# Reordering the opening of a two-layer macaron step: a split first modulation load, plain products moved up, a shared scaled x, a copy ahead of squares

## The chip, the cores and the metric

The kernel runs on one core of a Trainium2 chip. The metric is the device time of one execution in microseconds; the median over the runs of a program is compared. The profiler gives one execution of the program, with the span of its instructions and a record for each of them.

## What is computed

The reference is one inference step over two layers. Each layer is a half-step SwiGLU feed-forward block (FFN), a token mixer (differential attention, then multi-head latent attention), and a second half-step FFN. All sub-layers read a modulated RMS norm of the activations, and the modulation comes from a conditioning vector by a large matrix:

```python
def modulation(cond, w_mod, b_mod):
    m = jax.nn.silu(cond) @ w_mod + b_mod
    return m.reshape(cond.shape[0], 1, N_MOD, D_MODEL)

def modulate(x, g, shift, scale):
    return rms_norm(x, g) * (1.0 + scale) + shift

def swiglu(h, w_in, w_out):
    g, u = jnp.split(h @ w_in, 2, axis=-1)
    return (jax.nn.silu(g) * u) @ w_out
...
    x = x + m[2] * (0.5 * swiglu(modulate(x, norm_g[0], m[0], m[1]), w_in[0], w_out[0]))
```

There are 128 context tokens, with one conditioning vector, and 256 latent tokens with another. `D_MODEL` is 1024 and `D_FF` is 2816. Everything is float32. Only the first of these FFNs, and in it the first some 50 us, is touched by the change.

## The kernel before

Activations are held transposed as `x[128, 8, 384]`: eight tiles `k` of 128 features, 384 tokens, of which `LAT` (256 columns) are latent and `CTX` (128 columns) are context. A weight matrix is read from memory in panels; a panel `m` of the FFN's first matrix gives two output tiles (`half` 0 and 1) for each `k`. A float32 product is made of three faster ones: ScalarE (ACT) rounds a panel or an activation to a high part (`w_hi`, `hx_hi`), VectorE (DVE) subtracts to get the low part (`w_lo`, `hx_lo`), and TensorE (PE) adds hi*hi, hi*lo and lo*hi (`mm3`, lines 2367 to 2369).

**The opening** can't have all of this ready at once, since nothing is in SBUF when it starts. Three panels (`SLOTS`) are worked on together, tile `k` by tile `k`, as their data lands. The order of the work on each engine is written out by hand, one list for each engine, and semaphores tie the lists together:

- SyncE (SP) issues all loads of the opening on one DMA queue: `cond`, then the first modulation tile (`load_first(0)`, 1024 KB), x tiles 0 and 1, pieces of the three panels, modulation tiles 1 and 2, x tiles 2 and 3, and so on. The load of x tiles 4 to 7 (`x_in`) is the twelfth of the queue.
- For each `k`, TensorE computes the modulation of that tile: `mod_rows(k)` (line 2476, 16 records) from modulation tile `k`, then ScalarE copies the rows from PSUM to SBUF (`copied(k)`, line 973), then `mod_columns(k)` (line 2488, 4 records) turns them, and VectorE makes the gain from them (`gains_of(k)`, lines 1611 and 1544).
- For each `k`, x is scaled by that gain and multiplied by the three panels. For `k` = 0 that is done as plain float32 (`plain(m, 0, half)`, line 2498, two passes for each product), without a high and a low part. From `k` = 1 on ScalarE makes the high part of the scaled x (`xg_first(k)`, lines 985 and 987), VectorE the low part (`first_xg_low(k)`, lines 1628 and 1764), and TensorE does `tiles(m, k)`.
- Beside that runs the norm: ScalarE squares the eight x tiles (`square(k)`, line 967), VectorE adds them up (`add(k)`, line 1606), and TensorE sums over features (`sum_squares(0)`, line 2380) and later broadcasts the root (`broadcast(0)`). The panel products do not need the norm until their end: the result is scaled by it afterwards.

TensorE's place for `sum_squares(0)` is after `tiles(0, 3)`, behind two waits:

```python
tiles(0, 3)
pe.wait_ge(gains, 9)
sum_squares(0)
```

The ninth gain is the first instruction of `gains_of(4)` on VectorE, which stands behind `add(4)` to `add(7)` there. TensorE begins with `zeros(3)` (line 2521), products of a zero tile that keep it busy until the first data is in.

Of the kernel before, what the change touches and what calls it, by code (L numbers as in the profile page):

```python
# [21 lines left out]
F32 = mybir.dt.float32  # L22
F32R = mybir.dt.float32r
ALU = mybir.AluOpType
ACT = mybir.ActivationFunctionType
# [5 lines left out]
KD = D // P  # L31
KF = FF // P
T = 384
TX = T + 64
LAT = slice(0, 256)
CTX = slice(256, 384)
# [69 lines left out]
def build_step(nc, d, o):  # L106

    ctx = ExitStack()
    with ctx:
        def sem(name):  # L110
            return ctx.enter_context(nc.semaphore(name))
# [194 lines left out]
        wmf_loaded = [sem(f"wmf_loaded{i}") for i in range(KD)]  # L306
        condT_in = sem("condT_in")
        condT_ready = sem("condT_ready")
        first_in = [sem(f"first_in{i}") for i in range(5)]
        rows_ready = sem("rows_ready")  # L310
        rows_copied = sem("rows_copied")
# [353 lines left out]
        def _(sp):  # L665
# [25 lines left out]
            def load_first(k):  # L691
                sp.dma_start(wm_first[:, k], d["w_mod_first"][k]).then_inc(wmf_loaded[k], 16)
# [5 lines left out]
                sp.dma_start(w_raw[:, :, quarter(q)],  # L698
                             d["w_in"][0][0:SLOTS].rearrange("m p c -> p m c")[:, :, quarter(q)]).then_inc(first_in[q], 16)

            load_first(0)
            load_x(slice(0, 2), first_in[0])
            for cols, signal in ((slice(0, 2 * P), first_in[0]), (to_round(0), first_in[4])):
                sp.dma_start(w_raw[:, :, cols],
# [135 lines left out]
        def _(act):  # L840
# [115 lines left out]
            def first_norm():  # L956
# [5 lines left out]
                def square(k):  # L962
                    if k == 2:
                        act.wait_ge(first_in[1], 32)
                    elif k == 4:
                        act.wait_ge(x_in, 16)
                    nc.scalar.activation(squares_all[:, k, :], x[:, k, :], ACT.Square).then_inc(x_squared, 1)
# [8 lines left out]
                def xg_first(k):  # L976
                    if k == 0:
                        act.wait_ge(first_in[0], 32)
                    act.wait_ge(gains, 2 * k + 2)
                    if k < RAW:  # L980
                        nc.scalar.activation(xg_raw[:, k, LAT], x[:, k, LAT], ACT.Copy,
                                             scale=gmul[:, k, 1:2]).then_inc(xg_hi_done, 1)
                        return
                    out = hx_hi[:, k, :]
                    nc.scalar.activation(out[:, T:T + 2], modc[:, k, :], ACT.Copy)
                    for s, seg in SEGS:
                        ins = nc.scalar.activation(out[:, seg], x[:, k, seg], ACT.Copy, scale=gmul[:, k, s:s + 1])
                    ins.then_inc(xg_hi_done, 1)
# [30 lines left out]
                xg_first(2)  # L1019
                copied(3)  # L1020
                xg_first(3)
                square(4)
                square(5)
                copied(4)
                square(6)
                square(7)
                first_high(2)
                xg_first(4)
                copied(5)
# [456 lines left out]
        def _(v):  # L1486
# [109 lines left out]
            def first_norm():  # L1596
# [41 lines left out]
                first_low(0, (0, 1, 2))  # L1638
                add(1)
                gains_of(1)  # L1640
                first_xg_low(1)
                add(2)
                add(3)
                gains_of(2)
# [719 lines left out]
        def _(pe):  # L2364
# [70 lines left out]
            def ffn_in(f, n):  # L2435
# [32 lines left out]
                else:  # L2468

                    def mod_rows(k):  # L2470
                        pe.wait_ge(wmf_loaded[k], 16)
                        if k:
                            pe.wait_ge(rows_copied, k)
                        for i in range(2):
                            for g in range(4):
                                mm = nc.tensor.matmul(ps[32 * g:32 * g + 32, FIRST_ROWS, 0:2 * P],
                                                      condT[:, 4 * i + g, :], wm_first[:, k, 4 * i + g, :],
                                                      start=i == 0, stop=i == 1)
                        mm.then_inc(rows_ready, 1)
# [54 lines left out]
                    plain(0, 0, 0)  # L2534
                    plain(0, 0, 1)
                    plain(1, 0, 0)
                    mod_rows(1)
                    plain(1, 0, 1)
                    mod_columns(1)
                    plain(2, 0, 0)  # L2540
                    plain(2, 0, 1)
                    mod_rows(2)
                    tiles(0, 1)
                    mod_columns(2)
# [644 lines left out]
```

## Time and profile before

| | |
|---|---|
| median of 3 runs | 1514.74 us |
| lowest and highest | 1514.4 and 1515.72 us |
| the profiled execution | 1515.06 us |
| its span | 1513.1 us |
| TensorE busy | 1503.7 us, 99% of the span |
| VectorE, ScalarE busy | 1095.5 us, 676.1 us |
| TensorE busy between 1.90 and 51.00 us | 46.63 us of 49.10 |

The span runs from the first to the last instruction; the rest of the execution's time is around it. An engine's idle time in the profile stands in front of the instruction that ended it, with the instruction or the DMA that released it. Ends of matmuls are modelled, so the idle times of TensorE are good to about a tenth of a microsecond. Times in the trace count from the span's start.

### The profile page before, as it was taken

To read this page: it belongs to the slowest core of one execution; us is meant where nothing else is said; L and a number is where in the kernel's file an instruction comes from. 1 tells how busy PE (TensorE), PEld (TensorE's weight loads), DVE (VectorE), ACT (ScalarE), POOL (GpSimd) and SP (SyncE) were. 2 spreads that over 40 slices of the span, in tenths; PEclk is the share of its full clock that TensorE was granted. 3 is DMA by queue.
4 is the path that set the end of the run, shared out by engine and by line. 5 is a ranking of instruction groups with operands and counts; after the bars stand their busy time and mean duration, and the time that the engine had idled before them with its cause. 6 is when DMAs were issued, how large, how long until landed. Compare 5 with 4: busy or idle time off the path is not lost.

```text
span 1513.1 us, 22073 instructions
## 1 busy us (share of the span) xinstructions
PE 1503.7 (99%) x8874; PEld 1444.6 (95%) x8874; DVE 1095.5 (72%) x1788; ACT 676.1 (45%) x1067; POOL 34.8 (2%) x45
## 2 busy tenths in 40 slices
PE   8999999999999999999999999999999999999999
PEld 5999999988889999999999999999997899999999
DVE  4888899879887878776677887876588876343332
ACT  4633333353686633333363333325458765333221
POOL 0000000000031000000000000000030000000000
PEclk9999999999999999999999999999999999999999
DMA  9556667543133365655445555654331033333333
GB/s 378 225 217 241 246 243 255 185 149 135 73 99 140 131 230 209 236 188 190 169 177 203 215 224 204 239 181 153 115 121 57 5 136 112 139 114 136 101 130 118
DMA packets 53990, 258.02 MB, mean 171 GB/s; under 512 B 6656, under 2 KB 9728, under 8 KB 39168
## 3 DMA queue, kind: packets, MB, share of 16 engines
q1 hardware_dynamic: 51344, 253.13, 46.3%
q10 hardware_dynamic: 2544, 3.48, 0.7%
q8 instruction: 70, 1.15, 0.3%
q14 instruction: 32, 0.26, 0.1%
HBM read 253.29 MB, written 3.29 MB: 170 GB/s over the span
## 4 chain that ended last, share of the span: by engine, by line
PE 95%; DMA 2%; DVE 1%; ACT 1%; issue 1%; SPq 0%; DVEq 0%; ACTq 0%
PE ps L2367 29%; PE ps L2369 29%; PE ps L2368 29%; DMA x<-in_xT 1%; PE ps L3027 1%; PE ps L2918 1%; PE ps L3036 1%; PE ps L3050 1%; PE ps L2773 1%; PE ps L2742 1%; PE ps L2702 0%; PE ps L2760 0%; PE ps L2417 0%; DMA w_raw<-in_w_o 0%; PE ps L2380 0%
## 5 line engine op out<-in xcount | busy, mean ns | idle before, releaser
L1496 DVE TENSOR_TENSOR w_lo<-w_raw,w_hi 128x2048 fp32r<-128x2048 f32 (+3 forms) x176 | 345.4, 1964 | 222.7 <-ACT w_hi L848 220.2
L2367 PE MATMUL ps<-hx_hi,w_hi 128*128 128x384 f32 (+1 forms) x1434 | 481.2, 336 | 0.0
L2369 PE MATMUL ps<-hx_hi,w_lo 128*128 128x384 f32 (+1 forms) x1434 | 479.4, 334 | 0.0
L2368 PE MATMUL ps<-hx_lo,w_hi 128*128 128x384 f32 (+1 forms) x1434 | 479.4, 334 | 0.0
L848 ACT ACTIVATE w_hi<-w_raw 128x2048 fp32r<-128x2048 f32 (+3 forms) x176 | 290.8, 1653 | 390.6 <-DMA w_raw<-in_w_out 211.7
L2367 PEld LDWEIGHTS ps<-hx_hi,w_hi 128*128 128x128 f32 x1434 | 269.2, 188 | 2.5 <-issue 1.8
L2368 PEld LDWEIGHTS ps<-hx_lo,w_hi 128*128 128x128 f32 x1434 | 269.3, 188 | 0.0
L2369 PEld LDWEIGHTS ps<-hx_hi,w_lo 128*128 128x128 f32 x1434 | 269.2, 188 | 0.0
L2369 PE MATMUL ps<-g_hi,w_lo 128*128 128x384 f32 x704 | 236.6, 336 | 0.0
L2367 PE MATMUL ps<-g_hi,w_hi 128*128 128x384 f32 x704 | 236.5, 336 | 0.0
L2368 PE MATMUL ps<-g_lo,w_hi 128*128 128x384 f32 x704 | 236.5, 336 | 0.0
L1522 DVE SCALAR_TENSOR_TENSOR wm<-wm,cond 128x1024 f32<-128x1024 f32 x128 | 156.1, 1220 | 0.0
L1522 DVE SCALAR_TENSOR_TENSOR mod_prod<-wm,cond 128x1024 f32<-128x1024 f32 x128 | 156.1, 1220 | 0.0
L2369 PEld LDWEIGHTS ps<-g_hi,w_lo 128*128 128x128 f32 x704 | 132.4, 188 | 0.0
L2367 PEld LDWEIGHTS ps<-g_hi,w_hi 128*128 128x128 f32 x704 | 132.3, 188 | 0.0
L2368 PEld LDWEIGHTS ps<-g_lo,w_hi 128*128 128x128 f32 x704 | 132.3, 188 | 0.0
L2367 PE MATMUL ps<-w_hi,hx_hi 128*128 128x512 f32 (+2 forms) x306 | 113.9, 372 | 0.2 <-DVE hx_lo L1593 0.2
L2368 PE MATMUL ps<-w_lo,hx_hi 128*128 128x512 f32 (+2 forms) x306 | 110.8, 362 | 0.0
L2369 PE MATMUL ps<-w_hi,hx_lo 128*128 128x512 f32 (+2 forms) x306 | 110.8, 362 | 0.0
L1112 ACT ACTIVATE g_hi<-hf 128x384 fp32r<-128x384 f32 x79 | 41.6, 527 | 138.3 <-DVE hf L1850 138.3
L1831 DVE SCALAR_TENSOR_TENSOR x<-ps,gres,x 128x256 f32<-128x256 f32 x96 | 35.4, 413 | 88.0 <-PE ps L2369 88.0
L1110 ACT ACTIVATE hf<-ps 128x384 f32<-128x384 f32 x79 | 38.7, 490 | 121.8 <-PE ps L2369 121.8
(302 smaller groups left out, 1521.8 us busy)
## 6 DMA issues: line engine op xcount, KB each, us to landing
w_raw<-in_w_in SPq DMA_DIRECT2D x84, 1024.0 KB, 4.7
wm<-in_w_mod SPq DMA_DIRECT2D x128, 512.0 KB, 5.7
w_raw<-in_w_out SPq DMA_DIRECT2D x64, 704.0 KB, 4.1
w_raw<-in_w_qkv SPq DMA_DIRECT2D x12, 1024.0 KB, 4.7
wm_first<-in_w_mod_first SPq DMA_DIRECT2D x8, 1024.0 KB, 16.4
w_raw<-in_w_o SPq DMA_DIRECT2D x7, 1024.0 KB, 4.7
w_raw<-in_w_qup SPq DMA_DIRECT2D x8, 576.0 KB, 3.7
w_raw<-in_w_down SPq DMA_DIRECT2D x6, 704.0 KB, 4.1
```

Source lines behind the costliest of these rows:

```text
L848: nc.scalar.activation(w_hi[:, slot, 0:width], w_raw[:, slot, 0:width], ACT.Copy).then_inc(w_hi_done, 1)
L1110: nc.scalar.activation(sg[:, m % 2, :], ps[:, bank_pair(m), 0:T], ACT.Silu).then_inc(silu_done, 1)
L1112: nc.scalar.activation(g_hi[:, m, :], prod[:, m % 2, :], ACT.Copy).then_inc(g_hi_done, 1)
L1496: nc.vector.tensor_tensor(w_lo[:, slot, 0:width], w_raw[:, slot, 0:width], w_hi[:, slot, 0:width].bitcast(F32), ALU.subtract).then_inc(w_l ...
L1522: nc.vector.scalar_tensor_tensor(mod_prod[:] if s == 0 else panel, panel, 1.0, cond[:, s, :], ALU.mult, ALU.mult, accum_out=modc[:, q, s:s ...
L1831: ins = nc.vector.scalar_tensor_tensor(x[:, k, seg], ps[:, bank, seg], gres[:, k, s:s + 1], x[:, k, seg], ALU.mult, ALU.add)
L2367: nc.tensor.matmul(out, l_hi, r_hi, start=first, stop=False)
L2368: nc.tensor.matmul(out, l_hi, r_lo, start=False, stop=False)
L2369: return nc.tensor.matmul(out, l_lo, r_hi, start=False, stop=last)
L2742: mm = nc.tensor.matmul(ps[:, 2 * (u % 2) + c, 0:3 * P], qT, kT, start=term == 0, stop=term == 2)
L2773: mm = nc.tensor.matmul(ps[:, 7, j * P:(j + 1) * P], aT[:, u % 2, at + kb * P:at + (kb + 1) * P], v_all[:, slot, h * DIFF_VD:(h + 1) * DIF ...
L2918: mm = nc.tensor.transpose(ps[0:QK, TURN_BANK[t], i * P:(i + 1) * P], src, ident[:])
```

## The change

There are four edits in the opening, and none elsewhere.

1. The first modulation tile is loaded by two DMAs of half the size, with a semaphore each. TensorE's `mod_rows(0)` waits for the first half ahead of its first 8 records, and for the second ahead of the rest.
2. TensorE does `plain(1, 0, 1)` and `plain(2, 0, 0)` ahead of `mod_rows(1)`, and only `plain(2, 0, 1)` between it and `mod_columns(1)`.
3. For tile 1 the high part of the scaled x is shared: ScalarE makes the latent columns, VectorE the context columns and the two columns of the shift. VectorE waits on its own result (`first_ctx`) before it makes the low parts.
4. ScalarE does `copied(4)` ahead of the squares of tiles 4 to 7.

```diff
-            load_first(0)
+            sp.dma_start(wm_first[:, 0, 0:KD // 2], d["w_mod_first"][0][:, 0:KD // 2]).then_inc(half_mod_in, 16)
+            sp.dma_start(wm_first[:, 0, KD // 2:KD], d["w_mod_first"][0][:, KD // 2:KD]).then_inc(wmf_loaded[0], 16)
             load_x(slice(0, 2), first_in[0])
...
                     out = hx_hi[:, k, :]
+                    if k == 1:
+                        nc.scalar.activation(out[:, LAT], x[:, k, LAT], ACT.Copy,
+                                             scale=gmul[:, k, 1:2]).then_inc(xg_hi_done, 1)
+                        return
                     nc.scalar.activation(out[:, T:T + 2], modc[:, k, :], ACT.Copy)
...
                 xg_first(3)
-                square(4)
-                square(5)
                 copied(4)
-                square(6)
-                square(7)
+                for k in range(4, KD):
+                    square(k)
                 first_high(2)
...
                 gains_of(1)
-                first_xg_low(1)
+                nc.vector.tensor_copy(hx_hi[:, 1, T:T + 2], modc[:, 1, :])
+                nc.vector.tensor_scalar(hx_hi[:, 1, CTX], x[:, 1, CTX], gmul[:, 1, 0:1], None,
+                                        ALU.mult).then_inc(first_ctx, 1)
+                v.wait_ge(first_ctx, 1)
+                nc.vector.tensor_tensor(hx_lo[:, 1, T:T + 2], modc[:, 1, :], hx_hi[:, 1, T:T + 2].bitcast(F32),
+                                        ALU.subtract)
+                xg_low(0, 1)
                 add(2)
...
                     def mod_rows(k):
-                        pe.wait_ge(wmf_loaded[k], 16)
                         if k:
                             pe.wait_ge(rows_copied, k)
                         for i in range(2):
+                            if k == 0 and i == 0:
+                                pe.wait_ge(half_mod_in, 16)
+                            else:
+                                pe.wait_ge(wmf_loaded[k], 16)
                             for g in range(4):
...
                     plain(0, 0, 0)
                     plain(0, 0, 1)
                     plain(1, 0, 0)
+                    plain(1, 0, 1)
+                    plain(2, 0, 0)
                     mod_rows(1)
-                    plain(1, 0, 1)
+                    plain(2, 0, 1)
                     mod_columns(1)
-                    plain(2, 0, 0)
-                    plain(2, 0, 1)
                     mod_rows(2)
                     tiles(0, 1)
```

How the instructions stand on TensorE from the first `mod_rows` to the first product of tile 1, before (`wm_first` is the modulation tile, `mod_prod` holds the conditioning vector and the copied rows, `xg_raw` is the scaled x of tile 0; a row counts instructions as written, each of which shows as two records in the profile where it is plain float32):

```order
L2476 MATMUL ps<-wm_first,mod_prod 32x256 x8
L2488 MATMUL ps<-mod_prod 128x2 x2
L2521 MATMUL ps<-hn 128x384
L2498 MATMUL ps<-xg_raw,w_raw 128x386 x3
L2476 MATMUL ps<-wm_first,mod_prod 32x256 x8
L2498 MATMUL ps<-xg_raw,w_raw 128x386
L2488 MATMUL ps<-mod_prod 128x2 x2
L2498 MATMUL ps<-xg_raw,w_raw 128x386 x2
L2476 MATMUL ps<-wm_first,mod_prod 32x256 x8
L2367 MATMUL ps<-hx_hi,w_hi 128x386
```

And the same place in the changed kernel (its line numbers are 14 higher on these lines, and 11 higher on the last):

```order
L2490 MATMUL ps<-wm_first,mod_prod 32x256 x8
L2502 MATMUL ps<-mod_prod 128x2 x2
L2535 MATMUL ps<-hn 128x384
L2512 MATMUL ps<-xg_raw,w_raw 128x386 x5
L2490 MATMUL ps<-wm_first,mod_prod 32x256 x8
L2512 MATMUL ps<-xg_raw,w_raw 128x386
L2502 MATMUL ps<-mod_prod 128x2 x2
L2490 MATMUL ps<-wm_first,mod_prod 32x256 x8
L2378 MATMUL ps<-hx_hi,w_hi 128x386
```

Two plain products now stand ahead of the second `mod_rows`, and none is left between `mod_columns(1)` and `mod_rows(2)`.

On ScalarE, from the copy of rows 3 to the rounding of the third quarter of the panels, before (`mod_prod<-ps` is `copied`, `wm<-x` is `square`, `w_hi<-w_raw` is `first_high(2)`):

```order
L973 ACTIVATE mod_prod<-ps 128x256
L985 ACTIVATE hx_hi<-modc 128x2
L987 ACTIVATE hx_hi<-x,gmul 128x128
L987 ACTIVATE hx_hi<-x,gmul 128x256
L967 ACTIVATE wm<-x 128x384 x2
L973 ACTIVATE mod_prod<-ps 128x256
L967 ACTIVATE wm<-x 128x384 x2
L993 ACTIVATE w_hi<-w_raw 128x512 x3
```

And in the changed kernel:

```order
L976 ACTIVATE mod_prod<-ps 128x256
L992 ACTIVATE hx_hi<-modc 128x2
L994 ACTIVATE hx_hi<-x,gmul 128x128
L994 ACTIVATE hx_hi<-x,gmul 128x256
L976 ACTIVATE mod_prod<-ps 128x256
L970 ACTIVATE wm<-x 128x384 x4
L1000 ACTIVATE w_hi<-w_raw 128x512 x3
```

The copy of rows 4 no longer stands behind the first two squares, which need the load of x tiles 4 to 7.

On VectorE, from the gain of tile 1 to the next sums, in the changed kernel (before, rows 1646 and 1647 were not there):

```order
L1616 TENSOR_TENSOR modc<-ps,bmod 128x2x2
L1549 SCALAR_TENSOR_TENSOR gmul<-modc,norm_g 128x2
L1646 CAST hx_hi<-modc 128x2
L1647 TENSOR_SCALAR hx_hi<-x,gmul 128x128
L1650 TENSOR_TENSOR hx_lo<-modc,hx_hi 128x2
L1775 SCALAR_TENSOR_TENSOR hx_lo<-x,gmul,hx_hi 128x128
L1775 SCALAR_TENSOR_TENSOR hx_lo<-x,gmul,hx_hi 128x256
L1611 TENSOR_TENSOR sqacc<-sqacc,wm 128x384 x2
```

Two instructions of 2 and 128 columns came to VectorE, and went from ScalarE.

## Rows read from the trace of the kernel before

**Rows 1.** The page: span, and TensorE's busy time

```profile
span 1513.1 us, 22073 instructions
PE 1503.7 (99%) x8874; PEld 1444.6 (95%) x8874; DVE 1095.5 (72%) x1788; ACT 676.1 (45%) x1067; POOL 34.8 (2%) x45
```

**Rows 2.** Busy time by stage: stretch, length, engines, granted clock, DMA share, GB/s

```profile
1.90:26.42 24.52, 22.73 (x149) 13.81 (x150) 8.79 (x29) 10.30 (x26) 0.00 (x0) 1.00 1.01 390
1.90:51.00 49.10, 46.63 (x320) 34.82 (x321) 28.29 (x81) 29.29 (x71) 0.90 (x1) 1.00 0.81 315
```

**Rows 3.** The chain that ended last, opening: start, length, what

```profile
6.85 19.57 DMA x<-in_xT
26.45 0.53 ACT wm L967
...
29.70 0.81 PE ps L2380 x6
```

**Rows 4.** Timeline of TensorE: start, length, instruction, idle before and releaser

```profile
1.91 4.21 PE L2521 MATMUL ps<-hn 128*128 128x384 f32 x6 [1.91 <-POOL ident L765]
6.48 1.07 PE L2476 MATMUL ps<-wm_first,mod_prod 128*32 128x256 f32 x16 [0.36 <-DMA wm_first<-in_w_mod_first]
...
9.78 2.21 PE L2498 MATMUL ps<-xg_raw,w_raw 128*128 128x386 f32 x6 [0.37 <-ACT xg_raw L981]
12.53 1.07 PE L2476 MATMUL ps<-wm_first,mod_prod 128*32 128x256 f32 x16 [0.54 <-DMA wm_first<-in_w_mod_first]
...
14.28 0.50 PE L2488 MATMUL ps<-mod_prod 128*128 128x2 f32 x4
14.64 1.54 PE L2498 MATMUL ps<-xg_raw,w_raw 128*128 128x386 f32 x4
16.12 1.07 PE L2476 MATMUL ps<-wm_first,mod_prod 128*32 128x256 f32 x16
17.12 0.44 PE L2367 MATMUL ps<-hx_hi,w_hi 128*128 128x386 f32 x1
...
24.93 1.07 PE L2476 MATMUL ps<-wm_first,mod_prod 128*32 128x256 f32 x16
...
27.71 0.61 PE L2488 MATMUL ps<-mod_prod 128*128 128x2 f32 x4 [0.46 <-ACT mod_prod L973]
...
29.70 0.81 PE L2380 MATMUL ps<-ones,sqacc 128*128 128x1 f32 x6 [0.22 <-DVE modc L1611]
```

**Rows 5.** Timeline of SyncE's queue: when loads were issued

```profile
1.18 0.42 SPq L692 DMA_DIRECT2D wm_first<-in_w_mod_first  x1
...
2.12 1.31 SPq L704 DMA_DIRECT2D w_raw<-in_w_in  x2
```

**Rows 6.** DMA issues of single stretches: KB, us from issue to landing

```profile
mod_prod<-in_condT SPq DMA_DIRECT2D x1, 8.0 KB, 2.0
wm_first<-in_w_mod_first SPq DMA_DIRECT2D x1, 1024.0 KB, 5.2
w_raw<-in_w_in SPq DMA_DIRECT2D x1, 384.0 KB, 6.3
```

**Rows 7.** Timeline of ScalarE

```profile
9.22 0.51 ACT L981 ACTIVATE xg_raw<-x,gmul 128x256 f32<-128x256 f32 x1 [1.23 <-DVE gmul L1544]
...
15.32 0.78 ACT L987 ACTIVATE hx_hi<-x,gmul 128x128 fp32r<-128x128 f32 x2
...
27.29 0.37 ACT L973 ACTIVATE mod_prod<-ps 128x256 f32<-128x256 f32 x1
```

**Rows 8.** Timeline of VectorE

```profile
9.23 0.28 DVE L1636 TENSOR_SCALAR xg_raw<-x,gmul 128x128 f32<-128x128 f32 x1
...
16.21 0.16 DVE L1628 TENSOR_TENSOR hx_lo<-modc,hx_hi 128x2 fp32r<-128x2 f32 x1 [1.03 <-ACT hx_hi L987]
...
27.00 2.55 DVE L1606 TENSOR_TENSOR sqacc<-sqacc,wm 128x384 f32<-128x384 f32 x4 [0.92 <-ACT wm L967]
```

**Rows 9.** TensorE's waits over the whole span: total, times, longest

```profile
PE ps L2782 <- ACT aT L1200: 0.7, 1, 0.7
```

More of the change, by code:

```diff
@@ L308, in build_step @@
         condT_ready = sem("condT_ready")
+        half_mod_in = sem("half_mod_in")
+        first_ctx = sem("first_ctx")
         first_in = [sem(f"first_in{i}") for i in range(5)]
```

## The prediction

> **What bounds the kernel now.** I began with the page. Its first part gives TensorE 1503.7 us busy in a span of 1513.1 us [rows 1], so only waits of TensorE can be saved, and there are 9.4 us of them in all. The stage table then says where the change can reach: between 1.90 and 51.00 us TensorE is busy for 46.63 us [rows 2], so the opening holds 49.10 - 46.63 = 2.47 us of idle time in it. That would be the most that all four edits together could bring, if every wait went and nothing took its place.
>
> Next I read TensorE's timeline for the places of those waits [rows 4]. The reader is to see six: 0.36 us before the first modulation rows at 6.48 and 0.54 us before the second at 12.53 (both for a modulation load), 0.37 us before the first plain product at 9.78, 0.46 us before the record at 27.71 (for `copied(4)`), and 0.22 us before the sum of squares at 29.70, released by VectorE. One more of about half a microsecond, for `copied(0)`, makes up the 2.47 us.
>
> A sum of waits says nothing about which of them counts. For that I read the chain that ended last [rows 3], from its end backwards. It enters TensorE at 29.70 us, in `sum_squares(0)`. Ahead of that stand the four sums on VectorE, which start at 27.00 and take 2.55 us [rows 8], ahead of those the square of tile 4 on ScalarE at 26.45, and ahead of that one DMA: x tiles 4 to 7, issued at 6.85 and 19.57 us on its way [rows 3]. No instruction of TensorE before 29.70 us is in this chain. So TensorE passes 29.70 us when that load has landed (26.42 us) plus 3.28 us of squares, sums and one gain. What TensorE does earlier only has to be finished by then; whatever it gains before is waited away there.
>
> Why does the load take so long? Between 1.90 and 26.42 us the DMA engines are busy for a share of 1.01 at 390 GB/s [rows 2]. The load is the twelfth of its queue and stands behind nearly all of the 9.6 MB that this rate moves in 24.52 us. It is not held back by SyncE, which issued it 19.57 us before it landed. Only fewer bytes ahead of it or another order of the queue would bring it sooner, and the change does neither.
>
> **The change part by part.**
>
> *Two loads for the first modulation tile.* The one load of 1024 KB is issued at 1.18 [rows 5] and lands 5.2 us later [rows 6], at 6.38; the rows start at 6.48. Until 1.91 + 4.21 = 6.12 us TensorE is in the zero products [rows 4]. The first half lands no sooner than 1.18 + 2.0 us, the time of the load of 8 KB [rows 6], and no later than the whole did; so the first 8 records can start between 6.12 and 6.48, and I take 6.12, since 512 KB at 390 GB/s [rows 2] before the end of the whole is 5.1 us. The gain is then 0.36 us. The second half is in at 6.38, while the first 8 records still run. The first plain product moves from 9.78 to 9.42; the panel piece that it needs lands at 2.12 + 6.3 = 8.42 us [rows 5, 6].
>
> What does the extra load cost all those behind it? Their data waits in a full queue, so a later issue by some 0.4 us (the length of one issue [rows 5]) is hidden by the 19.57 us that the x load lies in it. What isn't hidden is work of the DMA engines for shorter pieces and one more completion. No row shows it. From below it is nothing; from above it is 2.0 us, the whole time of a load of 8 KB [rows 6], if no other load moved during it. But the twelve loads up to the x load had all landed by 26.42 us, with the engines busy all the time; at 2.0 us each for themselves, 24 us, they would have left 2.4 us for all those bytes. So it is near the lower end: I take 0.1 us, and keep 2.0 for the range.
>
> The rule that speaks against this edit is in the Trainium skill, "DMA: Bandwidth & Descriptors", section "Rules for kernel authors": at least 1 MiB in each DMA for full bandwidth; the section "Anatomy of one DMA" adds a constant of about 2.0 us for each. Where a load stands alone, the trace agrees with the constant (the 8 KB load took 2.0 us [rows 6]). Taken as a cost for each queued load it would make the sum +2.0 us in place of +0.1.
>
> *Two plain products ahead of the second rows.* A plain product takes 0.74 us (two of them from 14.64 to 16.12 [rows 4]). Five from 9.42 end at 13.12, so `mod_rows(1)` starts there and not at 12.53, when its tile is long in. Such a set of rows holds TensorE for 1.00 us (16.12 to 17.12 [rows 4]), so it ends at 14.12. One plain product brings TensorE to 14.86 for `mod_columns(1)`, which stood at 14.28: 0.58 us later, and the gain of tile 1 is later by as much. After 0.36 us (14.28 to 14.64) and 1.00 us of `mod_rows(2)` TensorE stands at 16.22 us and has nothing left to do until tile 1 is ready.
>
> *The shared scaled x.* Before, from `mod_columns(1)` to the first product of tile 1 it takes 17.12 - 14.28 = 2.84 us [rows 4], and TensorE covers that with two plain products and `mod_rows(2)`: 0.36 + 1.48 + 1.00 = 2.84. ScalarE's two pieces of tile 1 start at 15.32 and last 0.78 us, to 16.10 [rows 7], and VectorE begins its low part at 16.21 [rows 8]. Now ScalarE does only 256 columns, 0.51 us by the same shape for tile 0 [rows 7], and starts about 0.1 us sooner, as the shift's two columns went. VectorE's 128 columns take 0.28 us [rows 8] beside it, then come its wait on itself and the 0.16 us of the small low part. Both are done near 15.8 on the old clock, so the large low parts begin 0.4 to 0.5 us sooner. The chain is then about 2.4 us, and tile 1 starts at 14.86 + 2.4 = 17.26 us against 17.12: later by 0.14 us, with a new wait of about 1.0 us in front of it. From below, with nothing saved by sharing, it is 17.70, later by 0.58 us. What is queued behind VectorE's new wait are the low parts of tile 1 and `add(2)`, which has to wait for ScalarE's square of tile 2 anyway.
>
> *A copy ahead of the squares.* `mod_rows(4)` starts at 24.93 and takes 1.0 us [rows 4]; `copied(4)` can run at about 26.0 and is done in 0.37 us [rows 7], just before the x load lands at 26.42. Before, it ran at 27.29 behind two squares. So the 0.46 us wait before 27.71 goes. TensorE then arrives at `sum_squares(0)` 0.46 us earlier and waits 0.22 + 0.46 = 0.68 us there in place of 0.22: VectorE's four sums start with the square of tile 4 and are paced by VectorE, so they end when they did. If the rows came late, the copy would hold the first square by at most its 0.37 us; I take nothing, and keep the 0.37.
>
> *The sum.* On TensorE before 29.70 us the edits give +0.14 us at tile 1 and -0.46 us at 27.71. Both fall in front of the wait for the sums, which has 0.68 us of room with the copy moved. Even the +0.58 us fits. What is left is what moves the x load: +0.1 us. The profiled execution took 1515.06 us; with 0.1 that is 1515.2. It stood 0.3 us above the median of the three runs, 1514.74, so the median should be 1514.8 us.
>
> **The rivals.** First, *the gains get through*: the wait at 29.70 is 0.22 us long now, and if the x load landed 0.7 us sooner, TensorE would be what is late there, and the 0.46 + 0.22 = 0.68 us would be saved: 1514.1 us. For it speaks only that a load may land otherwise in other executions; against it, that before the change `copied(4)` stood behind the same load, so both kernels follow it.
>
> Second, *the constant for each load is paid in full*: 1514.74 + 2.0 = 1516.7 us. Against it stand the busy DMA engines of the opening.
>
> Third, ending on the slower side, *TensorE's clock falls* in the new wait of 1.0 us before tile 1. The granted clock is 1.00 in both stages [rows 2], that is 2.4 GHz, through waits of up to 0.54 us, and the longest wait for one cause after the start is 0.7 us in the whole span [rows 9]; so no row shows what 1.0 us does. At 1.2 GHz the work between 17.12 and 29.70, 12.58 - 0.68 = 11.9 us, takes twice as long; less the room of 0.68 it costs up to 11.2 us: 1526 us. It passes 0.2% when more than 0.68 + 3.0 = 3.7 us of work runs at the lower level. Against it: ahead of the new wait TensorE is busy from 9.42 to 16.22 us without a gap. The Trainium skill, "TensorE: Matmul & The Clock Gate", section "HAM oscillation — how this bites in real kernels", describes a kernel that fell back to half clock in each of its waits for a DMA; no run here has shown that yet.
>
> That the change does not do what it says is possible for the first edit (the zero products end at 6.12, and the half has to be in by then) and changes nothing in the time.
>
> **How the numbers follow.** The forecast has 0.88, the gains getting through 0.05, the full constant 0.03, the clock 0.03, and 0.01 is for something of which I know nothing. 0.2% of the time is 3.0 us, about what a measurement of this kernel can tell from no change; the three runs before lie 1.3 us apart. The first three cases are within it, the clock is beyond. So: faster 0.01, same 0.95, slower 0.04. The range reaches from the first rival less 0.5 us for the spread, 1513.6, to the second, 1516.7.
>
> **What would show it.** Right: the chain still comes through the x load at about 26.4 to 26.5 and enters TensorE in the sum of squares at 29.7 to 29.8; the wait in front of that is 0.5 to 0.9 us; the one before `mod_columns(4)` is gone; the first rows start near 6.1; a wait of 0.7 to 1.2 us stands before tile 1, at about 17.2. Wrong: the x load lands more than 1 us from 26.4 (another order or pace in the queue), the sums end sooner than 3 us after it, or a stretch shows a granted clock below 1.00 after 16 us.

## The result and the profile after

The changed kernel takes 1517.15 us (median of 22 runs, 1515.5 to 1518.98) against 1514.7 us (22 runs) before: a ratio of 1.0016, interval 1.0010 to 1.0022. That is 2.4 us slower, less than the 0.2% that I set as my bound, but clear of the noise and outside the range of the prediction, 1513.6 to 1516.7. The runs also spread over 3.5 us, where those of before spread over 2.2.

The page of the changed kernel, against [rows 1]:

```profile
span 1515.2 us, 22073 instructions
PE 1505.0 (99%) x8874; PEld 1445.4 (95%) x8874; DVE 1096.4 (72%) x1790; ACT 676.6 (45%) x1065; POOL 34.8 (2%) x45
```

The span grew by 2.1 us, TensorE's busy time by 1.3 us: it is busy longer with the same instructions. TensorE's timeline, against [rows 4] (start, length, instruction, idle before and releaser):

```profile
6.06 1.01 PE L2490 MATMUL ps<-wm_first,mod_prod 128*32 128x256 f32 x8
7.74 0.64 PE L2490 MATMUL ps<-wm_first,mod_prod 128*32 128x256 f32 x8 [0.67 <-DMA wm_first<-in_w_mod_first]
8.89 0.61 PE L2502 MATMUL ps<-mod_prod 128*128 128x2 f32 x4 [0.51 <-ACT mod_prod L976]
...
10.62 5.01 PE L2512 MATMUL ps<-xg_raw,w_raw 128*128 128x386 f32 x10 [0.37 <-ACT xg_raw L984]
15.56 1.07 PE L2490 MATMUL ps<-wm_first,mod_prod 128*32 128x256 f32 x16
...
19.60 0.45 PE L2378 MATMUL ps<-hx_hi,w_hi 128*128 128x386 f32 x1 [0.78 <-DVE hx_lo L1775]
...
27.17 1.07 PE L2490 MATMUL ps<-wm_first,mod_prod 128*32 128x256 f32 x16
...
31.83 0.81 PE L2391 MATMUL ps<-ones,sqacc 128*128 128x1 f32 x6 [0.84 <-DVE modc L1616]
```

The last row is `sum_squares(0)`: 31.83 us against 29.70. Everything after it takes what it took: span less this start is 1483.4 us in both kernels. So the whole loss lies ahead of it. It can be followed on these rows:

| piece | before | after | difference |
|---|---|---|---|
| start of the plain products | 9.78 | 10.62 | +0.84 |
| five plain products | | 4.94 us; 3.44 at full pace | +1.50 |
| start of tile 1 (the rest of the way) | 17.12 | 19.60 | +0.14 |
| tile 1 to `mod_rows(4)` | 7.81 us | 7.57 us | -0.24 |
| `mod_rows(4)` to the sum of squares | 4.77 us | 4.66 us | -0.11 |
| sum of squares | 29.70 | 31.83 | +2.13 |

(The 3.44 us is from 11.14 to 14.58 in a kernel kept busy, further below; the third line is what the first two leave of the 2.48 us by which tile 1 is late.) The plain products start late because of the first load. The landing of its two halves, issued at 1.18 and 1.65 (DMA issues: KB, us to landing), against [rows 6]:

```profile
wm_first<-in_w_mod_first SPq DMA_DIRECT2D x1, 512.0 KB, 4.2
wm_first<-in_w_mod_first SPq DMA_DIRECT2D x1, 512.0 KB, 6.0
```

The first half is in at 5.4 us, the second at 7.7, where the undivided tile was in at 6.38. The stage table of the changed kernel (stretch, length, engines, granted clock, DMA share, GB/s) shows both troubles:

```profile
4.00:6.00 2.00, 2.00 (x4) 0.67 (x2) 0.00 (x0) 0.00 (x0) 0.00 (x0) 1.00 0.80 297
6.00:8.00 2.00, 1.33 (x16) 0.36 (x16) 0.00 (x0) 0.00 (x0) 0.00 (x0) 1.00 0.91 319
8.00:10.00 2.00, 1.50 (x14) 0.74 (x6) 0.33 (x3) 0.39 (x1) 0.00 (x0) 1.00 1.05 369
10.00:12.00 2.00, 1.63 (x3) 0.84 (x3) 0.85 (x4) 1.45 (x5) 0.00 (x0) 0.57 1.04 437
12.00:14.00 2.00, 2.00 (x5) 1.16 (x4) 1.16 (x3) 0.91 (x3) 0.00 (x0) 0.58 0.98 415
14.00:16.00 2.00, 2.00 (x14) 0.90 (x16) 0.00 (x0) 0.00 (x0) 0.00 (x0) 1.00 0.97 395
```

The same table of the kernel before, for two of these stretches:

```profile
4.00:6.00 2.00, 2.00 (x4) 0.67 (x2) 0.00 (x0) 0.00 (x0) 0.00 (x0) 1.00 0.95 366
10.00:12.00 2.00, 1.99 (x6) 0.83 (x5) 1.23 (x4) 1.83 (x5) 0.00 (x0) 1.00 0.98 414
```

Between 4 and 6 us the DMA engines moved 297 GB/s and not 366, with a share of 0.80 and not 0.95; between 6 and 8 us 319, where before it was 369. And between 10 and 14 us the granted clock means 0.57, which is mostly the level of 1.2 GHz: it falls at about 10.3 us. Before that, TensorE had waited 0.67 and 0.51 us, and a third wait, of 0.37 us, was just beginning.

ScalarE and VectorE at the sums, against [rows 7, 8]:

```profile
28.31 0.38 ACT L976 ACTIVATE mod_prod<-ps 128x256 f32<-128x256 f32 x1 [0.90 <-PE ps L2490]
28.59 1.76 ACT L970 ACTIVATE wm<-x 128x384 f32<-128x384 f32 x4
...
29.14 2.55 DVE L1611 TENSOR_TENSOR sqacc<-sqacc,wm 128x384 f32<-128x384 f32 x4 [0.81 <-ACT wm L970]
```

The load of x tiles 4 to 7 landed 17.3 us after its issue at 8.65, at 25.95 us. The squares began 2.6 us later, at 28.59, because they stand behind `copied(4)`, which waited 0.90 us for TensorE's `mod_rows(4)`. The squares, once released by a load, are now released by TensorE.

### The profile page after: what moved, and what is told of

The parts are those of the page before. It is cut to its first block, busy times and chain, and to the rows that moved or that the text cites. A ratio compares the mean times of both kernels' runs of the same rounds, so it can differ in the third digit from the quotient of the medians.

```text
span 1515.2 us, 22073 instructions
## 1 busy us (share of the span) xinstructions
PE 1505.0 (99%) x8874; PEld 1445.4 (95%) x8874; DVE 1096.4 (72%) x1790; ACT 676.6 (45%) x1065; POOL 34.8 (2%) x45
## 4 chain that ended last, share of the span: by engine, by line
PE 96%; DVE 1%; ACT 1%; issue 1%; DMA 1%; SPq 0%; DVEq 0%; ACTq 0%
PE ps L2378 29%; PE ps L2379 29%; PE ps L2380 29%; PE ps L3041 1%; PE ps L2932 1%; PE ps L3050 1%; PE ps L3064 1%; PE ps L2787 1%; PE ps L2756 1%; PE ps L2490 0%; PE ps L2716 0%; DMA wm_first<-in_w_mod_first 0%; PE ps L2512 0%; PE ps L2774 0%; PE ps L2428 0%
```

## The experiments

All ratios are to the kernel before on the same chip, with 95% intervals. Each kernel's profile is one execution.

### One edit at a time

Four kernels, each the kernel before with one of the four edits of the diff above and nothing else.

> Only the first edit: the first modulation tile in two loads, everything else as before. Theory L (the loads): splitting slows the start of the DMA queue, so that the second half lands near 7.7 us and not 6.4, and TensorE starts everything behind it over 1 us later; the median rises by 1 to 2.5 us, with more spread between runs than before. Theory C (the clock): by itself the split also leaves TensorE with little work between 6 and 10.6 us, so the granted clock should show a stretch below 1.00 before 15 us; if the profile shows the late load but a clock of 1.00 throughout, the two are separate. Theory P (the plain products moved up are to blame): no change, within 0.3 us.

> Only the second edit: two plain products ahead of the second rows. Theory L and theory C: within 0.3 us of before, since tile 1 comes at most 0.6 us later, inside the wait for the sums. Theory P: 1 us or more slower, with tile 1 later than 17.8 us.

> Only the third edit: VectorE makes the context columns of the scaled x of tile 1. All theories: within 0.3 us of before; tile 1 starts up to 0.5 us sooner than 17.12 us, which the wait for the sums swallows.

> Only the fourth edit: the copy of rows 4 ahead of the squares of tiles 4 to 7. My prediction: within 0.3 us of before, the copy at about 26.0 us, just ahead of the landing of the x load, and a wait of about 0.7 us in front of the sum of squares. Theory S (the copy ties the squares to TensorE, whatever else happens): slower by 0.2 to 0.8 us, the squares starting behind a copy that ends after the x load has landed.

| edit alone | median | before | ratio | sum of squares at |
|---|---|---|---|---|
| 1, two loads | 1515.78 | 1514.86 | 1.0007 (0.9998 to 1.0016) | 29.44 us |
| 2, plains | 1514.93 | 1514.86 | 1.0002 (0.9993 to 1.0011) | 29.44 us |
| 3, share | 1514.99 | 1514.86 | 1.0002 (0.9994 to 1.0011) | 29.43 us |
| 4, copy | 1515.24 | 1514.86 | 1.0004 (0.9995 to 1.0013) | 30.08 us |

The second and third are free, as predicted. The split alone costs 0.9 us by the medians. In its profile the second half lands 6.0 us after its issue, at 7.64, with the clock at 1.00 throughout; so the late landing and the lost clock are separate things. But that execution, 1514.88 us, was the fastest of its eleven, and it passes the sum of squares at 29.44 us, sooner than the kernel before: there the late landing cost nothing. What the slower executions of this kernel do wasn't profiled.

With the plains alone, TensorE waited 1.06 us for the load and 1.30 us before tile 1, and the granted clock stayed at 1.00:

```profile
6.80 1.07 PE L2478 MATMUL ps<-wm_first,mod_prod 128*32 128x256 f32 x16 [1.06 <-DMA wm_first<-in_w_mod_first]
10.10 3.51 PE L2500 MATMUL ps<-xg_raw,w_raw 128*128 128x386 f32 x10 [0.38 <-ACT xg_raw L983]
18.09 0.45 PE L2369 MATMUL ps<-hx_hi,w_hi 128*128 128x386 f32 x1 [1.30 <-DVE hx_lo L1766]
```

The copy alone costs 0.4 us, and its profile says how. ScalarE with the copy alone:

```profile
26.56 0.38 ACT L975 ACTIVATE mod_prod<-ps 128x256 f32<-128x256 f32 x1 [0.91 <-PE ps L2476]
26.84 1.75 ACT L969 ACTIVATE wm<-x 128x384 f32<-128x384 f32 x4
```

The x load landed at 6.53 + 19.8 = 26.33 us; TensorE's first rows took 1.53 us in this execution and not 1.07, so all of TensorE was half a microsecond late, and the squares with it: 26.84. None of the four intervals excludes 1, so these four alone settle nothing but that no single edit costs 2.4 us. They add up to 1.5.

### One edit left out

> The whole change but its first edit: the first modulation tile in one load again. Theory L (the split is the cause): the first rows start near 6.6 us, plain products near 10, and the time falls back to within 0.6 us of before; what is left over is the copy ahead of the squares, which alone cost 0.4 us. Rival I (each edit costs its own part, split 0.9, copy 0.4, and the rest is chance): 1.3 to 1.5 us less than the whole change.

> The whole change but its fourth edit: the squares of tiles 4 and 5 ahead of the copy again. In the profile of the whole change the squares began at 28.59 us behind that copy, though the x load had landed at about 26. Theory S (the copy ties the squares to TensorE): the squares start when the load has landed, near 26, and the time is 0.5 to 1.2 us below the whole change. Rival: TensorE is itself so late that it passes the sum of squares no sooner, and nothing changes (less than 0.3 us).

> The whole change but its second edit: the plain products stand as before. With the split and the copy left in, theory M (all that makes TensorE late adds up once the copy ties the squares to it): the second rows start when their load is in, near 13.4 us, tile 1 about half a microsecond sooner than in the whole change, and the time is 0.4 to 0.8 us below it, that is 1.3 to 2.0 us above before. Rival: the plains moved up cost nothing, and it stays within 0.3 us of the whole change.

| left out | median | before | ratio |
|---|---|---|---|
| 1, two loads | 1515.93 | 1515.16 | 1.0003 (0.9994 to 1.0012) |
| 4, copy | 1516.33 | 1515.16 | 1.0009 (0.9999 to 1.0019) |
| 2, plains | 1516.78 | 1514.89 | 1.0012 (1.0003 to 1.0021) |

Leaving out the split or the copy takes away more than each cost alone (2.4 falls to 0.8 and to 1.2), which suggests that the two feed each other; but these two were timed on a chip on which the whole change was not, and the 0.8 us lies just outside the 0.6 of theory L. Without the copy TensorE goes through the sum of squares without a wait at 30.37 us, although its clock was lost in that profile too (0.76, 0.50 and 0.88 between 8 and 14 us). Without the plains the execution profiled had its second half in at 8.15 us and a TensorE at half pace until some 15 us. Its median is 1.9 us above before, within the 1.3 to 2.0 of theory M. Beside the whole change as timed on the same chip (1518.25 us, in the next part) it is 1.5 us faster, about twice what theory M gave, and the rival (within 0.3 us) is out. So the second edit, free by itself, is not free together with the split and the copy. How it costs there is not shown: the one profile of this kernel has a slow clock of its own.

### The clock

Two more products of zeros on TensorE, in the whole change:

```diff
+                            elif k == 0:
+                                zeros(1)
+                                pe.wait_ge(wmf_loaded[k], 16)
...
                     mod_rows(0)
+                    zeros(1)
                     mod_columns(0)
```

and, in a second kernel, only the split, with TensorE waiting for both halves at once.

> The whole change, with one more product of zeros on TensorE between the two halves of the first rows, and one between the first rows and the first columns, so that it does not wait there. Theory C (the lost clock is part of the price): the profile shows a granted clock of 1.00 from 8 to 16 us, the five plain products take 3.5 us and not 5.0, and the median is 0.5 to 1.3 us below the whole change. Rival: the clock's dip was a chance of one execution and the median stays within 0.3 us of the whole change.

> Only the first edit, but TensorE waits for both halves before its first rows, so that its work is as before and only the loads differ. Theory L: the second half lands 6.0 us after its issue as with the split alone, the first rows start near 7.6 us, and the time is within 0.3 us of the split alone (0.9 us above before). Rival: what cost 0.9 us was TensorE's rows in two pieces (a colder clock), and with one wait the time is that of before.

> The whole change kept busy, for a second time: theory C expects 1.0 to 1.4 us above before, against 2.4 and 3.3 us for the whole change as it is. If it was a chance of the first chip, it comes out above 2 us. The profile should again show full pace from the first rows on: the plain products 0.35 us a record.

> The whole change again, for its time beside the kernels of this chip and for a second profile. Theory C: the second half of the first load lands near 7.6 us again, the clock dips in some executions and not in others, so the times lie between 1515.5 and 1519 us. If this profile keeps the clock at 1.00, its span is 1 to 1.5 us shorter than the 1515.2 us of the first one.

Kept busy, the whole change took 1516.43 us, ratio 1.0008 (0.9998 to 1.0017), and a second time, on another chip, 1516.59, 1.0012 (1.0003 to 1.0021). The whole change as it is, timed again on that second chip, took 1518.25 us, 1.0019 (1.0010 to 1.0028), and showed the lost clock in its profile again (0.67 and 0.50 from 10 to 14 us). So 1.3 us above before stay in the one case and 1.7 in the other, out of 2.4 and 3.4 (only the second pair is from one chip). More work on TensorE made the kernel faster, with TensorE at full pace in those profiles from 8 to 16 us; no other part of the kernel was changed. The plain products, kept busy (second time):

```profile
11.14 3.51 PE L2515 MATMUL ps<-xg_raw,w_raw 128*128 128x386 f32 x10 [0.37 <-ACT xg_raw L984]
14.58 1.07 PE L2493 MATMUL ps<-wm_first,mod_prod 128*32 128x256 f32 x16
```

Ten records in 3.44 us against 4.94. With one wait for both halves TensorE was idle for 2.43 us ahead of its first rows, the granted clock fell shortly before 9 us and was back at about 15.5 us in the profile, and the time was 1516.96 us, ratio 1.0010 (1.0001 to 1.0019): 1.8 us and not the 0.9 of the split with two waits. Neither theory had said so. The loads are the same in both, so the difference, if it is more than chance (their runs overlap, on two chips), lies in what TensorE does while they are late; the lost clock is what the profile shows of it.

### The copy, with all else equal

Both kernels have the split, the plains, the share and the two products of zeros. They differ in the fourth edit alone.

> Edits one to three, the copy where it was, and two more products of zeros that keep TensorE busy in the first waits. Theory M with theory C: the clock's price and the copy's price are both gone, and what is left is TensorE being late by the second half of the load: 0.3 to 0.8 us above before. Rival (the split costs in another way than through TensorE's clock): 1.2 us or more above before.

Without the copy moved: 1515.15 us, ratio 1.0002 (0.9992 to 1.0011). With it (the second time above, same chip): 1516.59. The fourth edit costs 1.4 us here; seven of the eleven runs with it lie above all eleven without it. And what is left without it, 0.2 us, not clear of the noise and a little under the 0.3 to 0.8 expected, is the price of the other three edits when TensorE is kept busy: the late second half costs next to nothing by itself. TensorE, ScalarE and VectorE without it:

```profile
25.86 1.07 PE L2495 MATMUL ps<-wm_first,mod_prod 128*32 128x256 f32 x16
29.62 0.81 PE L2393 MATMUL ps<-ones,sqacc 128*128 128x1 f32 x6
...
26.00 0.92 ACT L970 ACTIVATE wm<-x 128x384 f32<-128x384 f32 x2
27.00 0.39 ACT L976 ACTIVATE mod_prod<-ps 128x256 f32<-128x256 f32 x1
```

and with it:

```profile
26.19 1.07 PE L2493 MATMUL ps<-wm_first,mod_prod 128*32 128x256 f32 x16
30.85 0.81 PE L2391 MATMUL ps<-ones,sqacc 128*128 128x1 f32 x6 [0.84 <-DVE modc L1616]
...
27.33 0.38 ACT L976 ACTIVATE mod_prod<-ps 128x256 f32<-128x256 f32 x1 [0.90 <-PE ps L2493]
27.61 1.75 ACT L970 ACTIVATE wm<-x 128x384 f32<-128x384 f32 x4
28.16 2.55 DVE L1611 TENSOR_TENSOR sqacc<-sqacc,wm 128x384 f32<-128x384 f32 x4 [0.81 <-ACT wm L970]
```

From `mod_rows(4)` to the sum of squares it is 3.76 us without the moved copy and 4.66 us with it. The 4.66 is a closed loop: rows, copy, square, four sums, gain. It is the same to the hundredth in the whole change (27.17 to 31.83), in its second profile (27.63 to 32.29) and with the copy alone (25.42 to 30.08), and each time TensorE waits 0.83 or 0.84 us in it. In the profile with the copy of this pair that wait was followed by a second loss. The granted clock behind it:

```profile
30.00:32.00 2.00, 1.16 (x9) 1.17 (x9) 1.83 (x6) 1.81 (x5) 0.00 (x0) 0.89 0.98 399
32.00:34.00 2.00, 2.00 (x10) 1.46 (x12) 1.70 (x6) 0.00 (x0) 0.90 (x1) 0.50 1.09 415
```

The clock fell 0.7 us after the end of that wait at 30.85 us. The span less the start of the sum of squares is 1516.7 - 30.85 = 1485.8 us here and 1483.4 in the kernel before, so this dip cost 2.4 us. It doesn't follow from the wait alone: in six other profiles with the moved copy the same wait of 0.83 or 0.84 us left the clock at 1.00 up to 36 us. This kernel's runs come in two groups, six up to 1516.6 us and five from 1517.9; without the copy all eleven lie between 1514.5 and 1516.0. That the upper group is the executions with this second dip fits, but only one of them was profiled. So of the 1.4 us, 0.9 is the longer loop, and the rest is most likely this dip.

### The other two edits together

> Edits two and three together, with the first load whole and the squares where they were. Theory M (the copy ties the sums to TensorE, the split makes TensorE late; the other two edits are nearly free): within 0.4 us of before. Rival (the plains moved up cost by themselves what they make tile 1 later): 0.6 us or more above before.

1515.11 us, ratio 1.0002 (0.9993 to 1.0010), on that same chip. Tile 1 came at 17.99 us, behind a wait of 0.77 us, and the squares still began when the x load was in, at 26.02. These two edits are not in the price as long as the first load is whole and the copy stands where it was.

### Why the second half lands late

Three kernels change the first load in turn; in d1 and d3 TensorE waits for both loads ahead of its first rows.

```diff
-            load_first(0)
+            # d1: halves of the partitions, rows of 8 KB
+            sp.dma_start(wm_first[0:P // 2, 0], d["w_mod_first"][0][0:P // 2]).then_inc(half_mod_in, 16)
+            sp.dma_start(wm_first[P // 2:P, 0], d["w_mod_first"][0][P // 2:P]).then_inc(wmf_loaded[0], 16)
+            # d2: one load, two rows of 4 KB for each partition
+            sp.dma_start(wm_first[:, 0].rearrange("p (h a) c -> p h (a c)", h=2),
+                         d["w_mod_first"][0:2, :, 0:KD // 2].rearrange("h p a c -> p h (a c)")).then_inc(wmf_loaded[0], 16)
+            # d3: one eighth and seven eighths
+            sp.dma_start(wm_first[:, 0, 0:1], d["w_mod_first"][0][:, 0:1]).then_inc(half_mod_in, 16)
+            sp.dma_start(wm_first[:, 0, 1:KD], d["w_mod_first"][0][:, 1:KD]).then_inc(wmf_loaded[0], 16)
```

> The kernel before, with the first modulation tile in two loads again, but one for each half of the partitions: the rows stay 8 KB long and not 4 KB, and TensorE waits for both. Theory K (the short rows make the start of the queue slow): both halves are in by 6.8 us and the time is within 0.3 us of before. Theory N (one more load at the head of the queue is what costs): the later half lands near 7.7 us as in every kernel with the split so far, and the time is 0.9 to 1.8 us above before.

> The kernel before, with one first load of 1024 KB as before, but fetched as two pieces of 4 KB for each partition (the second piece from the second modulation tile, so that part of the modulation is computed from the wrong weights; the amount of work is the same). Theory K (short rows): the load lands near 7.6 us in place of 6.4, and the time is that of the split with one wait, 0.9 to 1.8 us above before. Theory N (one more load): it lands near 6.4 us and the time is that of before.

> The kernel before, with the first modulation tile in two loads of one eighth and seven eighths; TensorE waits for both, and most bytes travel in rows of 7 KB. Theory N (one more load): the second lands near 7.6 us, 0.9 to 1.8 us above before. Theory K (short rows): it lands at 6.4 to 6.8 us, within 0.4 us of before.

The issues of d2, then of the second loads of d3 (issued at 1.64) and of d1 (at 1.78, one of two shown together, the mean of 5.6 and 7.5):

```profile
wm_first<-in_w_mod_first SPq DMA_DIRECT2D x1, 1024.0 KB, 6.4
```

```profile
wm_first<-in_w_mod_first SPq DMA_DIRECT2D x1, 896.0 KB, 6.8
```

```profile
wm_first<-in_w_mod_first SPq DMA_DIRECT2D x2, 512.0 KB, 6.5
```

One load with short rows (d2) is in at 1.18 + 6.4 = 7.6 us, just as late as the split, with not one load more: 1516.83 us, ratio 1.0010 (1.0000 to 1.0019). From 2 to 4 us its data moved at 242 GB/s, and from 4 to 6 us at 307, where before it is 312 and 366. So the number of loads is not needed for the delay; theory N as I put it falls. But seven eighths in rows of 7 KB (d3) is in only at 8.4 us: 1518.51 us, ratio 1.0019 (1.0009 to 1.0028). So theory K, which counted the bytes that travel in short rows, falls as well. What the split, d2 and d3 share is two rows for each partition in the first 1024 KB and not one. Halves of the partitions (d1) have one row for each, and were worst: the second half in at 9.3 us, 196 to 246 GB/s from 2 to 8 us, 1519.61 us, ratio 1.0028 (1.0018 to 1.0038). They must be slow for a reason of their own, presumably that half the partitions take the bytes at a time, which was not tried apart. What makes two rows slower at the head of this queue stays open.

### Versions that might beat both

The sum of squares one tile product later, with edits three and four, and the broadcast behind the third panel. The wait for the ninth gain stayed where it was, ahead of `tiles(1, 3)`:

```diff
                     pe.wait_ge(gains, 9)
+                    tiles(1, 3)
                     sum_squares(0)
-                    tiles(1, 3)
                     mod_rows(5)
+                    tiles(2, 3)
                     broadcast(0)
-                    tiles(2, 3)
```

> A version that might beat both: the kernel before with the third and fourth edits, and with TensorE's sum of squares one tile product later, behind the second panel of tile 3, and its broadcast behind the third. By the trace of before TensorE would then wait neither for the copy (0.46 us) nor for the sums (0.22 us): 0.3 to 0.7 us faster than before where TensorE is not late for another reason. Rival: TensorE is late often enough (clock, loads) that the copy holds the squares and the gain is gone: within 0.2 us of before.

And the kernel before with the third edit, and products of zeros of 128 columns, two ahead of the first rows, two ahead of the first columns and two ahead of the first plain product:

> A version that might beat both: the kernel before with the third edit, and with short products of zeros (128 columns) in TensorE's three waits before the first plain product. Theory C: the slow runs of before, those above 1515.5 us, come from a clock that rose late or fell in these waits, so they become fewer; the mean falls by 0.2 to 0.5 us, the median by 0.1 to 0.4. Rival: the fillers only delay TensorE, and the median rises by 0.1 to 0.3 us.

The first took 1516.31 us, ratio 1.0008 (0.9999 to 1.0017), 1.4 us above before: in its profile TensorE ran at half pace until some 15 us, and the copy at 28.43 us held the squares. TensorE waited for VectorE 0.82 us all the same, now ahead of the tile product:

```profile
31.93 0.45 PE L2377 MATMUL ps<-hx_hi,w_hi 128*128 128x386 f32 x1 [0.82 <-DVE modc L1615]
```

That follows from the edit, which moved the sum and not its wait for the ninth gain. So it doesn't test the idea behind it; whether a later sum together with its wait would gain is open. The second took 1514.81 us against 1514.91, ratio 0.9997 (0.9988 to 1.0006): its mean is 0.2 us lower and none of its eleven runs is above 1515.9, but that is not clear of the noise. No version was shown to beat the kernel before.

## Why the prediction was wrong

**What held.** The place of the bound was read rightly: the opening passes into the rest through the sum of squares, and the span less its start is 1483.4 us in both kernels. The first half was in before 6.12 us, and the first rows start at 6.06. The second and third edits cost nothing measurable together, as forecast. But the way to tile 1 was reckoned too long: by the prediction's numbers from the first plain product to tile 1 it is 17.26 - 9.42 = 7.84 us, and kept busy it is 18.61 - 11.14 = 7.47, against 7.34 before. Five plain products in a row take 3.44 us and not 3.70, and the chain from `mod_columns(1)` to tile 1 takes 2.28 us (16.33 to 18.61) and not 2.4. That the forecast's 0.14 is close to the measured 0.13 is luck, since the forecast started its way 0.36 us sooner.

**First step that failed, the size of a term.** "What isn't hidden is work of the DMA engines for shorter pieces and one more completion ... I take 0.1 us." The same part took the second half to be "in at 6.38". It lands at 7.7 (5.9 to 6.5 us after its issue in every kernel with this split). I had weighed the split only for the load at the end of the queue, which is indeed no later (25.95 us against 26.42), and not for the load at its head, where one row for each partition became two; why that is slower stays open. In place of 0.36 us sooner, the plain products start 0.84 us later. (The section "Anatomy of one DMA" that the prediction cites is about loads issued by GpSimd, and here SyncE issues them.)

**Second, a rival with the wrong trigger.** I put the fall of the clock into the new wait before tile 1, and gave it 0.03. It fell at about 10.3 us, after waits of 0.67 and 0.51 us and as one of 0.37 began, none longer than the 0.7 us of [rows 9]. The five plain products then took 1.50 us more. The wait before tile 1 came to 0.78 us here, and with the plains alone to 1.30 us, and behind neither did the clock fall. That a lost clock is paid as work at half pace was right; place and chance were wrong, and so was the sign to look for, a clock below 1.00 after 16 us. The Trainium skill, "TensorE: Matmul & The Clock Gate", section "HAM oscillation — how this bites in real kernels", describes a kernel whose engine fell back in each of its waits for a DMA. The traces agree in part: the clock was lost here behind one wait for a DMA (0.67 us) and one for ScalarE (0.51 us), and the two products of zeros took back 1.1 to 1.7 us; but with the plains alone a wait for a DMA of 1.06 us left it at full pace.

**Third, the room of 0.68 us was not there.** I wrote that both delays "fall in front of the wait for the sums, which has 0.68 us of room with the copy moved", and that a late copy "would hold the first square by at most its 0.37 us". But the wait at the sums is for VectorE, and with the copy ahead of the squares VectorE's sums depend on `mod_rows(4)`. A late copy doesn't hold the first square by its own length, but by all that TensorE is late. The room on that way was 4.77 - 4.66 = 0.11 us. Everything beyond that by which TensorE is late goes through copy, squares and sums and comes back to TensorE with 0.84 us of waiting on top. With the copy where it was, the same lateness of TensorE has 0.9 us less to pay (3.76 us against 4.66); shown by the pair that differs in this edit alone, 1515.15 against 1516.59 us. In the whole: of the 12.58 us from tile 1 to the sum of squares before, TensorE needs 31.83 - 19.60 = 12.23 with the copy moved, which leaves 0.35 us of room, and 30.37 - 19.03 = 11.34 without (the kernel without the fourth edit), which leaves 1.24. So of the 2.48 us by which tile 1 is late, 1.24 would have come through without the copy too, and the copy adds 0.89.

The sum as it should have been: +0.84 (second half), +1.50 in an execution that loses the clock, +0.14, less the 0.35 us that the old waits take up, is 2.13 us by the profile, and 2.4 us by the medians.

## What to carry to other kernels

The idle time in front of an instruction is room only for those that do not feed what it waits for: before an order is changed, follow the late engine's own results into that wait and take the shortest difference along the way. Moving an instruction that waits for a late engine ahead of work that waits only for a load ties the two together, and turns room into a loop; the copy that saved 0.46 us of one wait put 0.9 us more into another. Early in a kernel, short waits of TensorE can be followed by a lost clock that costs more than they do, so a load split to fill one wait must be checked for the waits that it makes.

## What the runs showed of the hardware

- A granted clock of 1.00 in the first microseconds is no proof of full pace. In the kernel before it stands beside six records of zeros of 384 columns that take 4.21 us [rows 4], where six of 386 columns later take 2.21. In the kernel without the second edit, TensorE's first six records of plain products:

```profile
12.09 3.39 PE L2512 MATMUL ps<-xg_raw,w_raw 128*128 128x386 f32 x6
```

The stage table gives 1.00 for 10 to 14 us there. The pace of like instructions is the safer reading; in the profiles of four kernels it stayed low until 14 to 18 us, once without the split.

- The clock fell at 9 to 11 us after two waits of 0.5 to 1.1 us each (both profiles of the whole change, and the one without the copy), and in one profile at 31.6 us, 0.7 us after a single wait of 0.84 us. The waits alone do not decide it: 1.06, 0.49 and 0.38 us ahead of the plain products left it at 1.00 with the plains alone, and so did 0.84 us ahead of the sum of squares in other profiles. What decides is not shown.
- The same 1024 KB at the head of a queue was in after 5.2 us with one row for each partition, after 6.4 us with two, and as two loads of 64 partitions each only 8.1 us after the first issue (from 1.18 to 9.3 us).
